# Two fused transformer blocks: a layer norm as a side task, another order of the modulation blocks, an uneven pace of the convolution

## The reference

```python
# first block (one layer)
mod_l = split(silu(c) @ w_mod + b_mod, 6)              # six vectors of 2048
mod_c = split(silu(c_ctx) @ w_mod + b_mod, 6)
hl = modulate(rms_norm(x), mod_l[0], mod_l[1]);  hc = modulate(rms_norm(ctx), mod_c[0], mod_c[1])
z = hl @ w_in + b_in                                   # conv a1,a2 | gating u,v | q | k | v | 3 gates
kc, vc = hc @ w_in[k, v columns]
y_na   = neighbourhood_attention(q, k, v, kc, vc, rpb) # 16 heads
y_conv = silu(layer_norm(depthwise_conv31(a1 * sigmoid(a2)) + conv_b)) @ w_conv_out
u, v_  = split(gelu(uv));  v_ = layer_norm(v_)         # the gating values' norm
y_sgu  = (u * (w_s . v_ + b_s)) @ w_sgu_out            # mixes tokens in chunks of 128
mix    = sigmoid(g1)*y_conv + sigmoid(g2)*y_sgu + sigmoid(g3)*(y_na @ w_na_out)
x = x + mod_l[2] * (mix @ w_o + b_o)
x = x + mod_l[5] * (relu(modulate(rms_norm(x), mod_l[3], mod_l[4]) @ w1 + b1)**2 @ w2 + b2)
# second block: differential attention, then pooling mixer, each with norms around it
```

## Time and profile before

| | |
|---|---|
| median of 3 runs | 2808.47 us |
| the profiled execution's own time | 2808.74 us |
| its span, first to last instruction | 2806.9 us |
| TensorE busy | 2705.8 us (96%) |
| VectorE busy | 1914.6 us (68%) |
| ScalarE busy | 1269.0 us (45%) |
| GpSimd busy | 188.1 us (7%) |
| moved by DMA | 539.02 MB, mean 192 GB/s |

### The profile page before, as it was taken

One profiled execution on the slowest core, in us unless ns is written; L12 is line 12 of the kernel. 1 busy time (PEld: TensorE's weight loads), 2 busy tenths in 40 slices (PEclk: granted clock), 3 DMA queues, 4 the chain that ended last, 5 costly groups with the idle time before them and its releaser, 6 DMA issues.

```text
span 2806.9 us, 51478 instructions
## 1 busy us (share of the span) xinstructions
PE 2705.8 (96%) x21438; PEld 2581.1 (92%) x21438; DVE 1914.6 (68%) x2951; ACT 1269.0 (45%) x1827; POOL 188.1 (7%) x180
## 2 busy tenths in 40 slices
PE   7999999899999999999999999999999998979996
PEld 4599977798999999999999999999999998979996
DVE  6765667789998777875555645677566656487564
ACT  5522344553444545544443434464444444444453
POOL 0000011000014000100000000030000000220011
PEclk9999999999999999999999999999999999989998
DMA  8766633456876777776555555554344443535563
GB/s 310 270 229 222 204 115 112 143 188 205 273 239 223 248 265 263 258 255 205 183 191 183 181 192 183 188 187 152 135 155 146 151 150 128 175 104 180 181 200 108
DMA packets 163991, 539.02 MB, mean 192 GB/s; under 512 B 31024, under 2 KB 35120, under 8 KB 163632
## 3 DMA queue, kind: packets, MB, share of 16 engines
q1 hardware_dynamic: 163760, 535.73, 57.3%
HBM read 533.57 MB, written 2.10 MB: 191 GB/s over the span
## 4 chain that ended last, share of the span: by engine, by line
PE 62%; DVE 5%; issue 1%; ACT 1%; POOL 0%; POOLq 0%; ACTq 0%; DVEq 0%
PE ps L531 20%; PE ps L536 19%; PE ps L533 19%; DVE lo L1570 1%; DVE row L2137 1%; PE ps L865 0%; DVE AL L2213 0%; PE ps L887 0%; PE ps L888 0%; PE ps L569 0%; DVE H L2221 0%; DVE ON L2145 0%; DVE Z L2301 0%; PE ps L960 0%; PE ps L959 0%
## 5 line engine op out<-in xcount | busy, mean ns | idle before, releaser
L986 ACT ACTIVATE hi<-raw 128x1024 fp32r<-128x1024 f32 x856 | 902.0, 1059 | 954.3 <-PE ps L536 463.2
L531 PE MATMUL ps<-AH,hi 128*128 128x256 f32 (+2 forms) x4480 | 1283.5, 287 | 13.7 <-DVE AL L2213 13.7
L536 PE MATMUL ps<-AH,lo 128*128 128x256 f32 (+2 forms) x4480 | 1270.4, 284 | 9.5 <-DVE lo L1570 9.5
L533 PE MATMUL ps<-AL,hi 128*128 128x256 f32 (+2 forms) x4480 | 1269.4, 283 | 0.0
L1570 DVE TENSOR_TENSOR lo<-raw,hi 128x1024 fp32r<-128x1024 f32 x856 | 1036.0, 1224 | 201.3 <-ACT hi L986 198.9
L531 PEld LDWEIGHTS ps<-AH,hi 128*128 128x128 f32 x4480 | 850.4, 190 | 45.8 <-issue 34.6
L536 PEld LDWEIGHTS ps<-AH,lo 128*128 128x128 f32 x4480 | 849.9, 190 | 12.3 <-DVE lo L1570 12.3
L533 PEld LDWEIGHTS ps<-AL,hi 128*128 128x128 f32 x4480 | 851.2, 190 | 1.0
L531 PE MATMUL ps<-YH,hi 128*128 128x256 f32 (+1 forms) x1536 | 433.8, 282 | 6.5 <-DVE YL L2148 6.5
L536 PE MATMUL ps<-YH,lo 128*128 128x256 f32 (+1 forms) x1536 | 432.9, 282 | 0.0
L533 PE MATMUL ps<-YL,hi 128*128 128x256 f32 (+1 forms) x1536 | 432.5, 282 | 0.0
(11 more groups left out here) (253 smaller groups left out, 2493.2 us busy)
## 6 DMA issues: line engine op xcount, KB each, us to landing
raw<-in_w_ff SPq DMA_DIRECT2D x256, 512.0 KB, 4.1
raw<-in_w_in SPq DMA_DIRECT2D x208, 512.0 KB, 4.4
raw<-in_w_mod SPq DMA_DIRECT2D x192, 512.0 KB, 4.7
raw<-in_w_ain SPq DMA_DIRECT2D x128, 512.0 KB, 3.6
raw<-in_w_pin SPq DMA_DIRECT2D x64, 512.0 KB, 3.5
raw<-in_w_o SPq DMA_DIRECT2D x32, 512.0 KB, 4.7
raw<-in_w_aout SPq DMA_DIRECT2D x32, 512.0 KB, 3.5
raw<-in_w_pout SPq DMA_DIRECT2D x32, 512.0 KB, 4.3
```

The costliest lines, as they stand in the source:

```text
L531: e.matmul(b.ap[:, o], hi[:, k, :], xh, start=start and k + i == 0, stop=False, skip_group_check=many)
L533: e.matmul(b.ap[:, o], hi[:, k, :], xl, start=False, stop=False, skip_group_check=many)
L536: mm = e.matmul(b.ap[:, o], los[j % NSPLIT][:, k, :], xh, start=False, stop=stop and k == KU - 1, skip_group_check=many)
L986: e.activation(his[u % NSPLIT][:, :, :], raws[raw_at[i]][:, :].rearrange("p (k m) -> p k m", k=KU), ACT.Copy).then_inc(s_hi, 1)
```

## The change

Three edits, all of order.

1. `finish(sn)` is gone on TensorE, ScalarE and VectorE, so the norm's steps are made one per unit between the following units of the linear unit, beside the convolution. The sync engine no longer waits for the norm before it loads w_s.
2. `unit_plan` places the 128 w_mod blocks otherwise. Before: 42 in keys and values (1.5 per unit), 58 in the three branches (two in five units), 28 in w_o and the feed-forward part (two in five). Now: 56 in keys and values (2 per unit), 32 in queries and gating values and 12 in the linear unit's first 12 units (1 per unit), none until w_o, and 28 from there on.
3. The convolution makes 2 and 3 taps in turn per tick, and none in ticks 26 to 48. Its number of ticks comes out as 122.

```diff
--- before.py
+++ after.py
@@ -58,7 +58,18 @@
 
 ROW = dict(x=0, ctx=1, sgv_m=2, sgv=3, cv_m=4, cv=5, s1=6, on=7, z=15, z2=16)
 
-CONV_TICKS, SGU_TICKS, PIN_TICKS = 124, 7, 9
+SGU_TICKS, PIN_TICKS = 7, 9
+
+
+def conv_steps(t):
+
+    return 0 if 26 <= t < 42 + SGU_TICKS else 2 + t % 2
+
+
+CONV_TICKS, _n = 0, 0
+while _n < 248:
+    _n += conv_steps(CONV_TICKS)
+    CONV_TICKS += 1
 
 GATES = (72, 88, 56)
 
@@ -147,10 +158,12 @@
             plan.append(("w_ff2", m, 2 * c))
             plan.append(("w_ff2", m, 2 * c + 1))
 
+
+    kv, q, glu, wo = NSTART, *(plan.index(u) for u in (("w_in", 32, 0), ("w_in", 0, 0), ("w_o", 0, 0)))
     out = []
     for i, u in enumerate(plan):
         out.append(u)
-        for _ in range(1 + i % 2 if NSTART <= i < 96 else 1 if i >= 176 and i % 5 < 2 + (i % 10 == 9) else 0):
+        for _ in range(2 if kv <= i < q else 1 if q <= i < glu + 12 or i >= wo and i % 5 < 2 else 0):
             if mod:
                 out.append(mod.pop(0))
     assert not mod and out.index(("mod", 19, 7)) < out.index(("w_conv", 14, 0))
@@ -489,7 +502,6 @@
                     bias_in(h)
             units(26)
 
-            e.wait_ge(s_vn, 8)
             e.wait_ge(s_na, 16)
             e.dma_start(WS, ar["sgu_w"]).then_inc(s_ws, 16)
             e.dma_start(BSr, ar["sgu_b"].partition_broadcast(128)).then_inc(s_bs, 16)
@@ -755,7 +767,6 @@
                 if m > 0:
                     gemm(lat, (s_gb, m + 1))
                 if m == 0:
-                    finish(sn)
                     cv = spawn(conv_means())
 
 
@@ -1837,11 +1847,14 @@
                 yield
 
             def convolve():
-                n = 0
+                t = n = 0
                 for m in range(8):
                     while m not in glued:
                         yield
                     for w in range(31):
+                        while n == conv_steps(t):
+                            yield
+                            t, n = t + 1, 0
                         s = col("conv_w", 8 * w + m)
                         if w == 0:
                             e.wait_ge(s_u, m + 1)
@@ -1855,9 +1868,7 @@
                         else:
                             o.then_inc(s_cv, 1)
                         n += 1
-                        if n % 2 == 0:
-                            yield
-                assert n == 2 * CONV_TICKS
+                yield
                 yield from layer_norm("cv_m", "cv")
                 for m in range(8):
                     y, z = tmp[3 + m % 2], tmp[5 + m % 2]
```

## The result

The changed kernel is slower. The median of its six executions is 2823.55 us, against 2809.41 for the kernel before on the same occasions. Five of the six took 2819.43 to 2827.41 us, with a median of 2822.21; the sixth, at 5383.8, is left out of the comparison. The ratio is 1.0048, with a 95% interval of 1.0037 to 1.0059: +13.5 us where I forecast -15.5. The profiled execution took 2819.43 us, its span is 2817.6.

The account below looks back on a forecast made before the run. TensorE, busy 96% of the span, was taken as the bound, so only its stops and slow clock could give time. From 2808.7 us, -10 + 4 - 6 - 9.5 + 6 + 0 = -15.5 gave 2793.2 us, range 2782 to 2807.

Parts of the forecast that it names:

- the failed step: Keys and values: two w_mod blocks per unit would cost nothing, 0 us, at most 4.
- part 1: Norm as a side task: removing the idle gap and slow clock gives -10 us; VectorE's added load costs +4.
- my slower rival: Attention becomes a serial chain, +32 us if 22 of 38 units are delayed, 2819 us in all; chance 0.11.
- +6: Attention, from queries and gating values on: added w_mod blocks overload VectorE and cost 6 us, bounds 0 and 14.
- the 6 that I named as a sign: Attention: TensorE's waits for PT, Pt or lo would sum to about 6 us; over 12 would refute the forecast.
- The norm and the pace: Norm beside the linear unit's units: -10 us; fewer taps around the gating stage's end: -6 us, bounds -2 and -8.
- The +4 for the norm's company: Linear unit: VectorE's norm work competes with taps and low parts and costs 4 us, bounds 0 and 8.
- a clock of 1.00 and no idle before the second sum: Norm: the trace after would show no idle over 1 us before its second sum, and a clock of 1.00.
- The rival that the norm stays on the path: Norm: in-order waits split the 8 us gap into several of 2, gain only 2, about 2801 us; chance 0.09.
- The branches: Branches: moving w_mod blocks out gives VectorE slack and saves 9.5 us, bounds -3 and -14.
- the sum: Whole kernel: -10 + 4 - 6 - 9.5 + 6 + 0 = -15.5 us, giving 2793.2 us.
- either price: Linear unit: each GpSimd addition delays VectorE 0.48 us by the profile row, or its full 0.73 by the skill's rule.

Follow-up runs that it names:

- the seven profiles with its order: The changed kernel and six follow-up variants of it with the same placement of w_mod blocks; their branches took 399.0 to 411.8 us.
- the version that looks further: Changed kernel with the planner's lookahead in keys and values raised by up to 4 w_mod blocks in place of 2: 2795.68 us, ratio 0.9962.
- the one with both steps late: Changed kernel with VectorE's value copies and w_mod sum additions in keys and values one unit later: 2802.77 us, ratio 0.9982.

## Why the prediction was wrong, step by step

**Keys and values: the failed step.** I wrote "**0**, at most 4", and argued from VectorE's sum (4.04 of 5.43 us), the DMA's rate and the buffers' time round. All three held: with the lookahead raised, VectorE is busy 71% of 120 us and the DMA moves 261 GB/s. None of them is what sets the pace. I left out the order. "Low parts are made three units ahead" stands in part 1 of the prediction, taken from the code's `AHEAD = 3`, and I did not ask whether it holds here. The reach is counted in blocks, and at two w_mod blocks per unit it shrinks to one unit (at 1.5 it was two, not three). With one unit ahead VectorE's in-order wait for a step of TensorE falls right in front of the part that TensorE needs. Measured in TensorE's stretch: +24.1 us, of them 1.9 for two more w_mod sums of 0.95, so 22 where I had 0; +2.5 when only the lookahead is raised, and +2.5 when only the two waiting steps are moved. The order of the changed kernel shows it: the copy that waits for s_vt stands one row ahead of every second low part. The rows of the order that I had read were those of attention and of the norm.

**Attention: my slower rival, and what it cost.** That rival had the right mechanism, two engines that take turns because of a fixed order, and the wrong place: attention, at a chance of 0.11. TensorE lost 15.1 us in attention. Four w_mod sums moved there, 3.8 us; that sums are moved and not added was right for the whole program. The other 11.3 stand against +6, inside my bounds of 0 and 14. TensorE's waits there, 332 to 540 us, are 8.1 us against 1.0 before. The three largest:

```profile
PE ps L722 <- DVE PT L1767: 2.8, 1, 2.8
PE ps L548 <- DVE lo L1580: 2.4, 2, 1.7
PE ps L543 <- ACT hi L997: 1.5, 1, 1.5
```

The waits for PT and low parts, 5.2 us, are about the 6 that I named as a sign. Part of the 11.3 comes from keys and values, whose lateness VectorE carries over: with 1.5 blocks there attention is 203.0 us, with five sums more than before, which leaves 5.3, and with the lookahead raised it leaves 8.1. How the rest divides is not shown.

**The norm and the pace: right alone. The +4 for the norm's company: too small.** Alone the norm brings 9.8 us, where I had 10, and the pace 6.3, where I had 6. The changed kernel gains 4.3 in that stretch, and 7.3 in the middle one of the seven profiles with its order (140.3 us). Less one sum that is 5.3 and 8.3, where I had 12. So VectorE's load beside the norm costs 8 to 11 us and not 4, at or above my upper bound of 8. I had expected a clock of 1.00 and no idle before the second sum. Windows after, and TensorE's waits from 548 to 960 us:

```profile
548.00:626.00 78.00, 72.95 (x592) 71.97 (x591) 74.67 (x119) 43.29 (x61) 5.82 (x8) 0.96 0.64 205
570.00:580.00 10.00, 6.36 (x36) 6.00 (x35) 8.09 (x11) 5.57 (x8) 3.02 (x4) 0.72 0.50 157
690.00:820.00 130.00, 129.04 (x1137) 128.84 (x1136) 113.38 (x191) 54.99 (x63) 0.00 (x0) 1.00 0.58 185
910.00:920.00 10.00, 8.22 (x56) 8.21 (x57) 4.75 (x4) 6.16 (x9) 3.13 (x3) 0.83 0.48 151
```

```profile
PE ps L581 <- POOL ssum L2330: 6.3, 2, 3.6
PE ps L548 <- DVE lo L1580: 5.9, 8, 1.0
PE ps L789 <- DVE tmp L1901: 1.9, 2, 1.6
```

There is still a stop of 3.6 us at the second sum, less than half of the 8.08 of the earlier trace rows, and the clock is 0.72 in that window. VectorE is busy 74.7 of 78 us in the linear unit (in attention 185.0 of 208.1, not near 100% as I had it), and GpSimd stands idle for 1.95 to 2.28 us before each pair of additions, waiting for squares, so the sums come late. The rival that the norm stays on the path was half right in kind. At the end of gating u 1.9 us of waiting are left of 6.7.

**The branches: right.** -19.0 in this pair of profiles and -16.8 for the middle one of the seven (403.8 us), of which 6.7 us are seven sums that left; 12.3 and 10.1 stand against 9.5. By the code there were 57 blocks in the branches before and 29 behind them, not 58 and 28. VectorE is busy 113.4 of 130 us, 87%, against 98%. The stop near 910 us is still there, 8.22 busy of 10 at a clock of 0.83, as I said of the conv norm's chain.

So one term, keys and values, was far out of its bounds, and the norm's company was at the edge or over it. The version with the deeper lookahead, 2795.7 us, is near where the sum pointed, 2793.2: 13.3 us below its own kernel before, where the sum had 15.5. Part of that closeness is luck. The loss beside the norm is larger than I put it, and in that profile the branches, at the low end of their spread, gain more.

Two slips in the prediction's working change nothing in the forecast. The rival that the norm doesn't leave the path sums to -2 + 4 - 6 - 9.5 + 6 = -7.5 and not to -5.5; its 2801 us are right. And VectorE's 5.54 us of waiting for the root begin at 514.2 us, ahead of the second sum, so they lie mostly in the 8.08 us gap and not behind it.

**GpSimd beside VectorE: smaller than either price.** GpSimd's squares met a full VectorE in the linear unit, as foreseen. The trace after has the same three taps without GpSimd at work and with two of its additions beside them:

```profile
558.04 1.52 DVE L1864 SCALAR_TENSOR_TENSOR CV<-U,vec,CV 128x256 f32<-128x256 f32 x3
...
565.72 2.25 DVE L1864 SCALAR_TENSOR_TENSOR CV<-U,vec,CV 128x256 f32<-128x256 f32 x3
...
565.99 1.70 POOL L2330 TENSOR_TENSOR ssum<-ssum,sqr 128x256 f32<-128x256 f32 x2 [1.95 <-ACT sqr L1018]
```

Two additions cost the taps 0.73 us. Over all seven, from 563.3 to 575.6 us, VectorE's instructions are 2.9 us longer than the same ones elsewhere, 0.4 us per addition, where the row had given 0.48. By the rule of the Trainium skill, "SBUF — State Buffer", section "SBUF: two separate sides", an addition could have held VectorE for its full length. That length is 0.85 us in the row of seven (5.93 / 7; the prediction has 0.73), so 6 us in all; the trace shows about half of that. It would fit if VectorE waited only for the rest of an addition already under way; that is not shown.

## What to carry to other kernels

Before adding load to a stage, work out how far ahead the producers run there in units of the consumer, not in entries of the list: here five entries were two units at 1.5 extra blocks per unit and one at 2. Where it falls to one, look in the new order for instructions that wait for the consumer and stand ahead of what it needs next; sums of busy time do not show these. And read the order of every stage that the edit touches, the ones with room first, since these are the ones that nobody watches. To say where the time went, mark the stages at instructions of the engine that sets the pace: marks on ScalarE showed a loss of 34.1 us here where TensorE had lost 24.1, and left a remainder in one experiment that was none.

## What the runs showed of the hardware

The start phase, with TensorE's instructions in the same order in every kernel here, took from 104.0 to 110.4 us to the first context product. In the profile of before the clock is 0.91 from 50 to 100 us and 0.96 in the next 50; in the one after it is 0.90 in the first 50 and 1.00 behind. That is up to 6 us between single profiles for no change at all, almost half of what was to be measured, so a difference of two profiles has to be taken stage by stage.

Even at a granted clock of 1.00 TensorE's pace isn't always the same. From 700 to 800 us the version that looks further and the one with both steps late are in the same stage, with the same order of units. Their windows:

```profile
700.00:800.00 100.00, 99.05 (x874) 98.85 (x873) 86.55 (x148) 42.15 (x48) 1.43 (x1) 1.00 0.55 180
...
700.00:800.00 100.00, 99.62 (x846) 99.42 (x845) 82.63 (x140) 41.58 (x47) 0.00 (x0) 1.00 0.53 173
```

Both are busy for over 99 us, but the first makes 874 matmuls and the second 846, 0.113 and 0.118 us of busy time each. Over the branches the two differ by 12.8 us. What sets the one or the other pace, no run here shows.
